# Hybrid decoder step: the mLSTM norm spread over the head loop, the SSM norm over the SSD groups, and the first output weights split a phase earlier

## The reference, cut to what matters

```python
h = rmsnorm(x, norm1_g) * (1 + sc1) + sh1              # sh, sc, g: six modulation vectors of w_ada
q, k, v, o, ig, fg, z, xbc, dt = jnp.split(h @ w_in, bounds, axis=-1)
qk, conv_a1 = causal_conv_silu(concat([q, k]), ...)    # 4 taps; k is scaled by 128 ** -0.5
(C1, n1, m1), h_a = lax.scan(mlstm_chunk, ...)         # 8 heads, 4 chunks of 128 tokens
# in mlstm_chunk: h = num / maximum(abs(den), exp(-m_t))
h_a = head_layernorm(h_a, mlstm_norm_g) * sigmoid(o)   # per head of 128 columns
xbc, conv_b1 = causal_conv_silu(xbc, ...)
S1, y_b = lax.scan(ssd_chunk, ...)                     # 16 heads
y_b = rmsnorm((y_b + d_skip * x) * silu(z), ssm_norm_g)
x = x + g1 * (concat([h_a, y_b]) @ w_out)
h2 = rmsnorm(x, norm2_g) * (1 + sc2) + sh2
x = x + g2 * peer_ffn(h2, w_query, sub_keys, peer_u, peer_v)
# head_layernorm: (h - mean(h)) * rsqrt(mean((h - mean(h)) ** 2) + EPS) * g
```

## Time and profile before

| | us |
|---|---|
| runs (median, lowest, highest) | 2517.42, 2515.47, 2517.84 |
| profiled execution | 2515.2 |
| its span | 2513.1 |
| TensorE busy | 2323.1 (92%) |
| VectorE busy | 1545.4 (61%) |
| ScalarE busy | 863.9 (34%) |
| POOL busy | 1138.6 (45%) |

### The profile page before, as it was taken

The page is one execution under the profiler, slowest core; times in us unless marked ns, Lnnn a source line. Parts: engine busy times, 40 slices in busy tenths (PEclk is TensorE's granted clock), DMA queues, the critical chain, the costliest instruction groups (busy, mean ns, idle before and its releaser), DMA issues.

```text
span 2513.1 us, 33256 instructions
## 1 busy us (share of the span) xinstructions
PE 2323.1 (92%) x12999; PEld 1971.7 (78%) x12999; DVE 1545.4 (61%) x2562; ACT 863.9 (34%) x1122; POOL 1138.6 (45%) x555
## 2 busy tenths in 40 slices
PE   5998988776996999999999989999999999999998
PEld 4998888654774987877877878888788888888886
DVE  4585557664443128778889887777365555555552
ACT  3424443342122133333234544455333232322221
POOL 1332235415442425565575665555564444444441
PEclk8999999986898999999999999999999999999999
DMA  7221212256634635555546787657565455555540
GB/s 262 68 84 53 65 60 68 80 152 204 196 123 151 152 78 139 140 149 128 150 116 170 212 258 215 194 156 213 211 259 185 189 200 200 200 187 197 193 157 34
DMA packets 313494, 392.67 MB, mean 156 GB/s; under 512 B 14490, under 2 KB 265774, under 8 KB 309003
## 3 DMA queue, kind: packets, MB, share of 16 engines
q1 hardware_dynamic: 218251, 302.86, 39.8%
q10 hardware_dynamic: 91664, 75.54, 9.2%
q0 software_dynamic: 3456, 12.58, 1.6%
HBM read 305.70 MB, written 81.26 MB: 154 GB/s over the span
## 4 chain that ended last, share of the span: by engine, by line
PE 54%; DVE 4%; POOL 2%; DMA 1%; ACT 1%; issue 1%; ACTq 0%; DVEq 0%
PE bank L2485 28%; PE bank L1942 22%; PE bank L2436 3%; DVE work L2162 2%; POOL utL_hid L1932 2%; DMA work<-sample_rows_dram 1%; DVE work L2165 1%; DVE ut_hid L1921 1%; PE bank L2441 1%; PE bank L2423 0%; POOL work L2120 0%; DVE work L2235 0%; ACT utH_hid L1928 0%; DMA work<-in_peer_u_dram,eu_sm 0%; POOL work L1863 0%
## 5 line engine op out<-in xcount | busy, mean ns | idle before, releaser
L1932 POOL TENSOR_TENSOR utL_hid<-ut_hid,utH_hid 128x1024 fp32r<-128x1024 f32 x128 | 349.0, 2726 | 328.9 <-ACT utH_hid L1928 328.3
L1942 PE MATMUL bank<-pH,utH_hid 128*128 128x512 f32 x1024 | 406.7, 397 | 13.4 <-POOL utL_hid L1932 13.4
L1942 PE MATMUL bank<-pH,utL_hid 128*128 128x512 f32 x1024 | 399.7, 390 | 0.0
L1942 PE MATMUL bank<-pL,utH_hid 128*128 128x512 f32 x1024 | 399.5, 390 | 0.0
L2485 PE MATMUL bank<-area,work 128*128 128x512 f32 x1536 | 350.8, 389 | 0.0
L2485 PEld LDWEIGHTS bank<-area,work 128*128 128x128 f32 x1536 | 288.3, 188 | 59.9
L857 PE MATMUL ps_in<-hH_in,wH_in 128*128 128x260 f32 x816 | 241.1, 296 | 18.1 <-POOL wL_in L813 16.7
L1921 DVE STREAM_TRANSPOSE ut_hid<-u_hid 128x1024 f32<-128x1024 f32 x128 | 158.8, 1241 | 146.1 <-POOL utL_hid L1932 127.7
L813 POOL TENSOR_TENSOR wL_in<-wb_in,wH_in 128x1024 fp32r<-128x1024 f32 x52 | 128.3, 2468 | 261.8 <-ACT wH_in L770 261.8
L2098 POOL TENSOR_TENSOR pL<-work,pH 128x1024 fp32r<-128x1024 f32 x64 | 155.7, 2434 | 190.7 <-ACT pH L2341 190.7
L1942 PEld LDWEIGHTS bank<-pH,utH_hid 128*128 128x128 f32 x1024 | 193.0, 188 | 56.3 <-POOL utL_hid L1932 18.6
(11 more groups left out here) (515 smaller groups left out, 4447.7 us busy)
## 6 DMA issues: line engine op xcount, KB each, us to landing
u_hid<-in_peer_u_dram SPq DMA_DIRECT2D x256, 256.0 KB, 5.2
work<-in_peer_v_dram SPq DMA_DIRECT2D x64, 1024.0 KB, 4.9
hidden_dram<-ge_hid ACTq DMA_DIRECT2D x64, 512.0 KB, 3.2
gates_dram<-area ACTq DMA_DIRECT2D x16, 2048.0 KB, 10.1
wb_in<-in_w_in_dram SPq DMA_DIRECT2D x26, 1024.0 KB, 5.3
wm_ml<-in_w_ada_dram SPq DMA_DIRECT2D x32, 512.0 KB, 4.0
raw_out<-in_w_out_dram SPq DMA_DIRECT2D x16, 1024.0 KB, 5.3
area<-hidden_dram SPq DMA_DIRECT2D x16, 1024.0 KB, 6.8
```

The costliest lines, as they stand in the source:

```text
L1932: self.nc.gpsimd.tensor_tensor(self.utL[:, u % 2], self.ut[:, u % 2], self.utH[:, u % 2].bitcast(F32), ALU.subtract).then_inc(self.low, 1)
L1942: mm = self.nc.tensor.matmul(self.pa[u % 2][:, :], w[:, u % 2, k, :], x[:, k, :], start=(n == 0), stop=(n == 3 * KD - 1))
```

## The change

In `front_phase` the order of the chunks is another: four chunks of v stand behind the xbc chunks (two ahead of `first_z`, two behind it), and the last two of o at the very end. The SSM norm's squares and sums follow each SSD group (`z_done`) and use other scratch; the root comes three chunks earlier; KSCALE is done by ScalarE instead of POOL.

In `mlstm_phase` the norm works on pairs of heads g (4 x 128 elements of a head an instruction). The pairs 0 to 2 are done inside the head loop, one pair behind it: denominators and centring in even heads, variances in both, the root and the factor in odd ones. The division by the denominator is taken into the factor. POOL multiplies with the factor (`scale`). Heads 0 to 3 are turned (`give`), evicted (`take`) and split inside the loop at heads 4 to 7. Pair 3 and heads 4 to 7 stand behind it, between the 16 modulation blocks. The `wm` buffers lie in a common area `R.wstage` with the first two w_out tiles, which are loaded when the last blocks are done; the first is split in this phase.

In `out_phase` these steps are dropped from the start, the numerator's matmuls stand between those of a product, mean, variance and heads of the samples come one to two half steps later, and the last eight tiles are `wide`: two rows of w_out per partition, 4 KB each, instead of eight pieces of 1 KB.

```diff
-    chunks = [(2 * D + c * P, NV + c, "copy", c) for c in range(8)]
+    values = [(2 * D + c * P, NV + c, "copy", c) for c in range(8)]
+    out_gates = [(3 * D + c * P, NO + c, ACT.Sigmoid, c) for c in range(8)]
+    chunks = values[0:4]
...
+    chunks += values[4:6]
     first_z = len(chunks)
+    chunks += values[6:8]
     chunks += [(Z0 + c * P, NZ + c, ACT.Silu, c) for c in range(8)]
-    chunks += [(3 * D + c * P, NO + c, ACT.Sigmoid, c) for c in range(8)]
+    chunks += out_gates[0:6]
     chunks += [(c * P, NQ + c, "conv", (c, V_CAW + c, 16, V_CAB + c)) for c in range(16)]
+    chunks += out_gates[6:8]
...
+        z_sum = S.rb[:, 0:T]
+        z_sq = lambda f: z_sum if f == 0 else y[:, f % 2, :] if f < 6 else S.proj[:, NX + f - 6, 0:T]
+        z_done = {first_z + 4 * (f // 2) + 4: (f, f + 1) for f in range(0, KD, 2)}
+        Z_ROOT, Z_NORM, Z_GAIN = first_q + 4, first_q + 5, first_q + 6
...
+                    x = S.proj[:, slot, 0:T]
+                    silu = nc.scalar.activation(x, y[:, convs(n) % 2, :], ACT.Silu)
+                    if first_k <= n < first_k + 8:
+                        own(silu)
+                        silu = nc.scalar.activation(x, x, ACT.Copy, scale=KSCALE)
+                    silu.then_inc(used, 1)
...
+                for k in z_done.get(n - 1, ()):
+                    act.wait_ge(X.m["t_out"], k + 1)
+                    if k > 2:
+                        act.wait_ge(z_added, k - 2)
+                    nc.scalar.activation(z_sq(k), z(k), ACT.Square).then_inc(z_squared, 1)
...
                     dve.wait_ge(used, c - 1)
+                if c in (12, 13):
+                    dve.wait_ge(z_added, c - 8)
                 dve.wait_ge(by_dve, before(n + 1, False))
```

The mLSTM phase, first TensorE, then ScalarE:

```diff
+            def give(f, to):
+                pe.wait_ge(normed, f + 1)
+                if 0 < f < 4:
+                    pe.wait_ge(hmoved, f)
+                for c in range(NC):
+                    mm = nc.tensor.transpose(to[:, c * L:(c + 1) * L], num[:, c, f, 0:P], S.ident[:, :])
+                mm.then_inc(hturned, 1)
...
+                    if c == 1 and h in OUT_AT:
+                        pe.wait_ge(kv_ready, min(h + 2, H_A))
+                        give(OUT_AT[h], trv)
...
+            pe.wait_ge(c_ready, NC * H_A)
+            nc.tensor.transpose(mb[0:H_A, 0:P], C[:, :, P], S.ident[:, :]).then_inc(n_out, 1)
+            for f in (4, 5):
+                modulation(2 * f + 8)
+                modulation(2 * f + 9)
+                give(f, qk[f % 2])
             pe.wait_ge(num_ready, NC * H_A)
-            for g in range(4):
+            pe.wait_ge(hmoved, 4)
+            for g in range(7):
+                modulation(20 + g)
                 tails(g)
-            for c in range(16, 26):
+            for c in range(27, MODS):
                 modulation(c)
-                if 18 <= c < 21:
-                    tails(c - 14)
-            pe.wait_ge(normed, 1)
-            for h in range(H_A):
-                if h >= 2:
-                    pe.wait_ge(hmoved, h - 1)
-                for c in range(NC):
-                    mm = nc.tensor.transpose(qk[h % 2][:, c * L:(c + 1) * L], num[:, c, h, 0:P], S.ident[:, :])
-                mm.then_inc(hturned, 1)
-                if h < 6:
-                    modulation(26 + h)
             mod_turn(MODS - 1)
+            for f in (6, 7):
+                pe.wait_ge(hmoved, f - 1)
+                give(f, qk[f % 2])
...
+            def square(f):
+                act.wait_ge(centred, f + 1)
+                if f >= 2:
+                    act.wait_ge(var_ready, f - 1)
+                nc.scalar.activation(sq[f % 2][:, :, :], head(f), ACT.Square).then_inc(squared, 1)
+
+            def root(g):
+                act.wait_ge(scored_var, g + 1)
+                own(nc.scalar.activation(pair(var, g), pair(var, g), ACT.Ln))
+                nc.scalar.activation(pair(var, g), pair(var, g), ACT.Exp, scale=-0.5).then_inc(rooted, 1)
...
                     if c == 1 and h + 1 < H_A:
                         exponentials(h + 1)
                     if c % 2:
                         modulation(2 * h + c // 2)
+                    if g >= 0 and h % 2 == 0 and c >= 2:
+                        square(2 * g + c - 2)
+                    if g >= 0 and h % 2 and c == 1:
+                        root(g)
+                    if c == 3 and h in OUT_AT:
+                        high(OUT_AT[h])
                 if h >= 6:
...
+            for c in range(16, 18):
+                modulation(c)
+            square(6)
+            square(7)
...
-            for g in range(4):
+            high(4)
+            for c in range(18, 20):
+                modulation(c)
+            high(5)
+            root(3)
+            for g in range(7):
+                modulation(20 + g)
...
+            for c in range(27, MODS):
                 modulation(c)
-                if c - 26 < H_A:
-                    high(c - 26)
-            for h in range(MODS - 26, H_A):
-                high(h)
+            high(6)
+            high(7)
+            act.wait_ge(conv_out, 16 * 6)
+            act.wait_ge(w_first, 16)
+            for v in range(2):
+                nc.scalar.activation(R.wH[v], R.raw[0][:, :, v * P:(v + 1) * P].rearrange("p (a b) n -> p a b n", a=2), ACT.Copy).then_inc(w_high, 1)
...
+            def scale(f):
+                pool.wait_ge(factor, f // 2 + 1)
+                v.tensor_tensor(head(f), head(f), bcast(var[:, :, f], 2, P), ALU.mult).then_inc(normed, 1)
```

VectorE and SP (the new helpers stand as the change has them):

```diff
+            def denominators(g):
+                dve.wait_ge(num_ready, NC * (2 * g + 2))
+                last = num[:, :, 2 * g:2 * g + 2, P]
+                own(V.scalar_tensor_tensor(out=pair(den, g), in0=last, scalar=-1.0, in1=last, op0=ALU.mult, op1=ALU.max))
+                own(V.tensor_tensor(pair(den, g), pair(den, g), S.cols[:, :, 3, 2 * g:2 * g + 2], ALU.max))
+                V.reciprocal(pair(r, g), pair(den, g))
+
+            def centre(f):
+                own(V.reduce_sum(mean[:, :, f], head(f), AX_X))
+                own(V.tensor_scalar(mean[:, :, f], mean[:, :, f], 1.0 / P, None, ALU.mult))
+                V.tensor_tensor(head(f), head(f), bcast(mean[:, :, f], 2, P), ALU.subtract).then_inc(centred, 1)
+
+            def variance(f):
+                dve.wait_ge(squared, f + 1)
+                V.reduce_sum(var[:, :, f], sq[f % 2][:, :, :], AX_X).then_inc(var_ready, 1)
+
+            def scaled_variance(g):
+                dve.wait_ge(var_ready, 2 * g + 2)
+                own(V.tensor_tensor(pair(var, g), pair(var, g), pair(r, g), ALU.mult))
+                own(V.tensor_tensor(pair(var, g), pair(var, g), pair(r, g), ALU.mult))
+                V.tensor_scalar(pair(var, g), pair(var, g), 1.0 / P, EPS, ALU.mult, ALU.add).then_inc(scored_var, 1)
+
+            def factors(g):
+                dve.wait_ge(rooted, g + 1)
+                V.tensor_tensor(pair(var, g), pair(var, g), pair(r, g), ALU.mult).then_inc(factor, 1)
+
+            def take(f, bank_):
+                dve.wait_ge(hturned, f + 1)
+                V.scalar_tensor_tensor(out=S.proj[:, NQ + f, 0:T], in0=bank_[:, :], scalar=S.vec[:, V_GA + f:V_GA + f + 1],
+                                       in1=S.proj[:, NO + f, 0:T], op0=ALU.mult, op1=ALU.mult).then_inc(hmoved, 1)
...
+                    if g >= 0 and h % 2 == 0:
+                        if c == 0:
+                            denominators(g)
+                        if c in (1, 2):
+                            centre(2 * g + c - 1)
+                        if c == 3:
+                            variance(2 * g)
+                    if g >= 0 and h % 2:
+                        if c == 0:
+                            variance(2 * g + 1)
+                            scaled_variance(g)
+                        if c == 2:
+                            factors(g)
+                    if c == 2 and h in OUT_AT:
+                        take(OUT_AT[h], trv)
...
-            dve.wait_ge(num_ready, NC * H_A)
-            own(V.scalar_tensor_tensor(out=den[:, :, :], in0=num[:, :, :, P], scalar=-1.0, in1=num[:, :, :, P], op0=ALU.mult, op1=ALU.max))
-            own(V.tensor_tensor(den[:, :, :], den[:, :, :], S.cols[:, :, 3, 0:H_A], ALU.max))
-            own(V.reciprocal(r[:, :, :], den[:, :, :]))
-            for c in range(NC):
-                h_c = num[:, c, :, 0:P]
-                own(V.tensor_tensor(h_c, h_c, bcast(r[:, c, :], 2, P), ALU.mult))
-                own(V.reduce_sum(mean[:, c, :], h_c, AX_X))
-                own(V.tensor_scalar(mean[:, c, :], mean[:, c, :], 1.0 / P, None, ALU.mult))
-                V.tensor_tensor(h_c, h_c, bcast(mean[:, c, :], 2, P), ALU.subtract).then_inc(centred, 1)
-                dve.wait_ge(squared, c + 1)
-                V.reduce_sum(var[:, c, :], sq[:, :, :], AX_X).then_inc(var_ready, 1)
-            dve.wait_ge(var_ready, NC)
-            V.tensor_scalar(var[:, :, :], var[:, :, :], 1.0 / P, EPS, ALU.mult, ALU.add).then_inc(var_ready, 1)
```

(38 more changed lines are left out.)

172 lines of the change are left out of this document (82 added, 90 removed).

## The result

The changed kernel takes 2498.5 us (median; 2496.1 to 2503.2) against 2517.6 us before: a ratio of 0.9927, 95% interval 0.991 to 0.9945, faster by 0.7%. Its profiled execution has a span of 2495.8 us. The forecast was 2484 (2464 to 2504): the sign and the range held, the gain was 19 us and not 33.

What follows compares the result with a forecast made beforehand. TensorE and VectorE not covering each other in the last projections, and latency behind the head loop, were taken as bounds; front -19.5, loop +18, behind it -3, output -28 sum to -32.5 from 2515.2: 2482.7, said as 2484 (2464 to 2504).

Steps and rivals of the forecast that it cites:

- (a): Front: first convolution four value chunks earlier, gain 12 us. Output phase: first weight tiles ready early, half 4 earlier, -11 us.
- (b): Front: 15 chunks nearer their pace, squares moved, KSCALE on ScalarE, gain 14.5 us. Output phase: numerators between products, -12 us.
- (c): Front: two sigmoid chunks now end the phase, +7 us. Output phase: later mean and variance sums don't hold TensorE, -4 us.
- Head loop: mLSTM head loop: the norm of heads 0 to 5 enters it and is partly hidden, +18 us (0 to +36).
- Behind the loop: Stretch behind the mLSTM head loop: 54 instead of 57 us, the modulation blocks' chain replacing the norm, -3 us (-9 to +5).
- Output phase: Output phase: early weights, interleaved numerators, later sample sums and wider weight loads together, -28 us (-14 to -36).
- (d): Output phase: the last eight weight tiles come in rows of 4 KB instead of 1 KB, -1 us (0 to -3).
- R2: Output phase: transfers bound it, POOL's waits for states surface by 14 us, so it gives 14 only: 2498 us; chance 0.15.
- R1: Head loop: centring fits into the wait for ti, only roots leak, cost 8 instead of 18 us: 2474 us; chance 0.20.
- R3: Front gives 5 instead of 19.5 us: early convolutions meet gate work, z products slow the passes: 2499 us; chance 0.10.
- R5: Whole kernel: gains and the loop's growth cancel, loop and output phase at their poor ends, no change: 2517 us; chance 0.03.
- R4: Head loop bound by VectorE in series with POOL: 63 us added in place of 18, slower, 2529 us; chance 0.05.

Runs made afterwards that it cites:

- the second combination: Changed kernel with norm behind the loop, z products and sample work later, SSM states' decays and samples' root another half step later: 2473.5 us, ratio 0.9826.

## Why the prediction was right in sign and too large

**Front, -19.5 said, -17.3 measured.** (a) The first q copy comes 13.7 us earlier (12 said). (b) 15 copies take 99.6 us (341.00 to 440.58) instead of 108.6, a gain of 9.0 where I took 14.5: "what stays is the Ln/Exp pair (4 us)" was too small. The pair also holds back a low part on POOL; moving that gave 3.7 us of it in one profile. A new wait of 5.1 us came too, at 111 us, where the gates' exponentials stand ahead of a high part. (c) +5.4 instead of +7. Read as a cost of the last two chunks this would mislead: undoing it made the kernel slower, and TensorE's gap at the phase's end was 6.4 and 7.1 us instead of 2.6. The reading that fits is that the chunks cost the same anywhere and at the end cover the convolution's tail.

**Head loop, +18 said, +20.2 measured.** The roots were priced rightly (2.5 us each; 2.5 to 2.6). But the walk left out the clock. The waits of TensorE grew by 10.6 us (C 6.5, `take` 2.9, the bank of an earlier `num` 1.4, less 0.2), and its busy time by 9.6, of which 3.4 are the new turns; the other 6.2 are old matmuls at a granted clock of 0.89 instead of 1.00. The sum came near because I counted centring, evictions and turns at some 10 of the 17.4, and the centring alone cost 2.5 in the run without it. On the table load the trace decided rightly: 2.94 us from the first load to `ti`, four instructions without a drain between them, where the Trainium skill (ScalarE: Activation LUTs, What ACT_TABLE_LOAD costs) would have 2.66 for each of the two switches.

**Behind the loop, -3 said, -5.6 measured.** I said 54 us and it is 52.9; the rest of the gap is the stretch before, 58.5 us from the turn of C's column to the first transpose and not 57. The chain of the modulation blocks did take the norm's place: two waits of 3.6 and 2.6 us for ScalarE's copy, then seven blocks with tails. The two low parts of the weights cost 4.6 us at the very end.

**Output phase, -28 said, -11.4 measured: the step that failed.** (a) Half 4 came 9.2 us earlier (11 said). (b) From the start of half 4 to the end of half 11, the half steps with the numerators in or behind them, it is 51.1 us before and 49.9 after: a gain of 1.2 where I took 12. "Perhaps one weight load in four hides behind a 512-column product" was wrong: at full clock 32 interleaved matmuls add 3.5 us to a half step (6.6 instead of 3.0), and in a block in the kernel before they took little more:

```profile
643.81 3.73 PE L1399 MATMUL pm_sm<-projarea,state 128*128 128x1 f32 x32
```

What interleaving does avoid, slow products behind each block, it gave back in halves 4 and 5, where everything ran at half clock. (c) No gain instead of 4: from the end of half 11 to the end of the products it is 73.1 us before and 73.2 after. The waits for the mean and variance (4.9 and 1.5) are nearly gone, and waits of 2.8, 1.8 and 0.6 us for low parts, the second with a slow half step behind it (4.6 us), stand there. (d) -1.1, as said. Together 9.2 + 1.2 - 0.1 + 1.1 = 11.4.

**The rivals.** R2 gave 2498 (chance 0.15), and the median is 2498.5. Its mechanism was shown in two runs: with later sample work POOL waited 14.4 us for a state ahead of a low part, and with decays and root out of the way the products fell from 137.1 to 124.9 us. The run with the low part first doesn't show it, since VectorE's queue held TensorE there. And the number fits partly by chance: in the changed kernel low parts cost 9.5 us of waits, not the 14 that I gave R2, and the failed interleaving carries the rest. I wrote "2 to 5 us of waits, already in (b)'s share"; this was too low, since I let TensorE come 11 us earlier and left the first state's landing where it was. R1, R3 and R5 did not happen. R4 (VectorE in series with POOL) asked for a loop 50 us longer; it grew by 20.2, and centring, 9.3 us of VectorE's work, cost 2.5. But the slow small operations beside POOL that R4 named do appear in the output phase, where I did not look for them.

What stays open: which part of the loop's other 9 us (20.2 less 8.7 and 2.5) belongs to turns, evictions and squares, and how the output phase's loss divides between the states' landing, POOL's order and VectorE's copies. No run took them out alone.

## What to carry to other kernels

Before moving work into a loop that is bound by a chain through three engines, ask what stands ahead of the chain's link in each queue; a root with two table loads costs its full length there, 2.5 us idle of TensorE each, and a slower clock behind it. An earlier start of the bound engine is worth only as much as its next supplier keeps up: here low parts behind a queue of decays, whose first state could be worked on only 8.2 us into the phase, made it wait 9.5 us, until the sample work was moved three half steps later and low parts ahead of decays. And test the parts apart: the new front and output phases with the early weights were worth 30 us around the old loop, the whole change 19.

## What the runs showed of the hardware

A stretch full of short waits has no fixed time. The changed loop, the same code each time, took 75.8, 78.4, 79.8 and 81.2 us at granted clocks of 0.89, 0.85, 0.83 and 0.82, with nearly the same waits (for C 9.7 us in the first, 9.5 in the second); three more profiles have 75.0 to 75.6. The window of the slowest (the run with all of o ahead of q and k):

```profile
467.65:548.83 81.18, 66.43 (x580) 55.58 (x580) 47.97 (x148) 42.17 (x104) 13.62 (x12) 0.82 0.37 106
```

The old loop, with no wait of TensorE over 1.1 us for its C, took 55.6 us in four of five profiles and 57.1 in the fifth. So single profiles of kernels with the changed loop differ by some us, and an edit worth 3 or 4 us in one stage, as the z products', doesn't show in the medians.

Small copies of VectorE took ten times as long beside POOL. The output phase has six (64x64 and 64x8 elements) ahead of VectorE's first addition to a state. In the changed kernel's profile they took 0.15 to 0.19 us each, while POOL waited for the first state; its decays began 8.2 us into the phase, right behind them. In the run with the z products later they began after 7.2 us, and all six copies took 1.89 to 1.96 us, about as long as one decay (1.9):

```profile
606.07 1.89 DVE L1617 COPY dec_sm<-bb_out 64x64 f32<-64x64 f32 x1
616.28 1.22 PE L1492 MATMUL pv_sm<-vrow,pick_out 64*128 64x512 f32 x2 [6.16 <-DVE state L1633]
```

In that profile TensorE waited 6.2 us for VectorE in place of the 4.3 for the low part, and the products took 146.2 us instead of 142.6. The seven profiles with this output phase go the same way: where the decays began 7.7 us or later into the phase, at most one copy was slow; where they began after 7.2 to 7.4 us, four to six were, and TensorE waited 2.6 to 6.2 us for VectorE. No run moved the copies out of POOL's way.

At half clock 12 products and 32 interleaved one-column matmuls took 12.3 us and the clock did not come back within them; in the second combination the first such half step began at full clock and stayed there (6.6 us, 607.77 to 614.33).
